# Two mixing slots handed to expert weights earlier, and an undivided gather, in a two-layer trunk kernel

## What is computed

```python
for l in range(DEPTH):                       # 2 layers; x is 256 x 1024, float32
    h = rms_norm(x, norm_mix_g[l])
    x = x + token_mixers(h, ...)             # h @ w_in, three branches, gates, w_proj_*, w_out
    h = rms_norm(x, norm_ffn_g[l])
    x = x + hier_moe(h, ...)                 # top-1 of 4 groups, top-2 of its 8 experts, 32 experts
return rms_norm(x, norm_final_g)

# in token_mixers, for branches i = a, b, c
merged = g[i = 0] * (ya @ w_proj_a) + g[1] * (yb @ w_proj_b) + g[2] * (yc @ w_proj_c)
return merged @ w_out
# in hier_moe, for each expert e, on its tokens
hid = silu(xb @ w_gate[e]) * (xb @ w_up[e]);  out += (hid @ w_down[e]) * weight
```

## Time and profile before

| what | value |
|---|---|
| median of 3 runs | 1387.93 us (1385.76 to 1388.62) |
| the profiled execution, its own time | 1388.38 us |
| its span, first to last instruction | 1385.9 us |
| mean granted TensorE clock | 0.996 of full |
| TensorE busy | 1367.3 us, 99% |
| VectorE, ScalarE busy | 584.4 us, 386.0 us |
| moved by DMA | 490.26 MB, 354 GB/s over the span |
| waits of TensorE for a DMA | 0.9 us in all, once |

### The profile page before, as it was taken

The page is one execution under the profiler, slowest core; times in us unless marked ns, Lnnn a source line. Parts: engine busy times, 40 slices in busy tenths (PEclk is TensorE's granted clock), DMA queues, the critical chain, the costliest instruction groups (busy, mean ns, idle before and its releaser), DMA issues. The chain is left out here.

```text
span 1385.9 us, 18830 instructions
## 1 busy us (share of the span) xinstructions
PE 1367.3 (99%) x7801; PEld 803.3 (58%) x7801; DVE 584.4 (42%) x945; ACT 386.0 (28%) x707; POOL 16.6 (1%) x44
## 2 busy tenths in 40 slices
PE   9999999999999999999999999999999999999997
PEld 8899888544444444444488988884444444444442
DVE  7796646632222222222278956466222222222223
ACT  6555443211111111111164553441111111111112
POOL 0000000100000000000000000010000000000000
PEclk9999999999999999999999999999999999999999
DMA  9645668999999999999975557599999999999996
GB/s 307 225 166 184 245 227 313 413 405 427 426 427 428 428 426 427 429 426 420 406 239 187 213 186 269 184 381 397 420 424 429 428 427 427 428 426 429 424 421 256
DMA packets 89676, 490.26 MB, mean 354 GB/s; under 512 B 10686, under 2 KB 13816, under 8 KB 58872
## 3 DMA queue, kind: packets, MB, share of 16 engines
q1 hardware_dynamic: 89488, 489.03, 87.9%
q10 hardware_dynamic: 104, 0.03, 0.0%
HBM read 487.99 MB, written 1.05 MB: 353 GB/s over the span
## 5 line engine op out<-in xcount | busy, mean ns | idle before, releaser
L2172 PE MATMUL psB<-slots,uT 128*64 128x512 f32 x2016 | 455.7, 595 | 0.3 <-DVE uT L1588 0.2
L2172 PEld LDWEIGHTS psB<-slots,uT 128*64 128x64 f32 x2016 | 140.3, 137 | 263.8 <-issue 259.9
L2182 PE MATMUL psC<-slots,ybT_plain 128*64 128x512 f32 x1024 | 233.0, 598 | 1.6 <-DMA slots<-in_expert_w_down_dram 0.9
L1249 DVE TENSOR_TENSOR parts<-slots,parts 128x2048 fp32r<-128x2048 f32 (+1 forms) x80 | 177.7, 2249 | 70.1 <-ACT parts L1006 69.2
L1006 ACT ACTIVATE parts<-slots 128x2048 fp32r<-128x2048 f32 (+1 forms) x80 | 148.3, 1888 | 98.0 <-PE psB L1817 52.5
L1645 DVE TENSOR_TENSOR x<-x,psA 128x1024 f32<-128x1024 f32 x60 | 73.3, 1222 | 211.9 <-PE psA L2222 211.9
L1113 ACT ACTIVATE rel_parts<-psC 128x512 fp32r<-128x512 f32 x62 | 37.1, 598 | 385.5 <-PE psC L2182 210.5
L1817 PE MATMUL psB<-parts,hT_parts 128*128 128x512 f32 x448 | 139.0, 391 | 0.9 <-DVE tmp L1526 0.5
L2182 PEld LDWEIGHTS psC<-slots,ybT_plain 128*64 128x64 f32 x1024 | 68.8, 136 | 117.5 <-issue 111.3
L1588 DVE TENSOR_TENSOR uT<-psA,g_ffn 128x512 f32<-128x512 f32 x64 | 44.3, 692 | 163.1 <-PE psA L2133 162.8
L1817 PE MATMUL psA<-parts,hT_parts 128*128 128x512 f32 x320 | 99.5, 392 | 0.0
(11 more groups left out here) (373 smaller groups left out, 1379.1 us busy)
## 6 DMA issues: line engine op xcount, KB each, us to landing
slots<-in_expert_w_down_dram SPq DMA_DIRECT2D x44, 2048.0 KB, 22.5
slots<-in_expert_w_gate_dram SPq DMA_DIRECT2D x40, 2048.0 KB, 22.9
slots<-in_expert_w_up_dram SPq DMA_DIRECT2D x40, 2048.0 KB, 21.7
slots<-in_w_in_dram SPq DMA_DIRECT2D x56, 1024.0 KB, 5.2
slots<-in_expert_w_gate_dram SPq DMA_DIRECT2D x44, 1024.0 KB, 10.5
slots<-in_expert_w_up_dram SPq DMA_DIRECT2D x42, 1024.0 KB, 10.5
slots<-in_expert_w_down_dram SPq DMA_DIRECT2D x28, 1024.0 KB, 10.7
slots<-in_expert_w_down_dram SPq DMA_DIRECT2D x24, 512.0 KB, 10.4
```

Source lines behind the costliest of these rows:

```text
L1249: v.tensor_tensor(low_part, mix_slot(i), high_part, ALU.subtract).then_inc(low_dve, 1)
L2172: ins = te.matmul(psB[j * BLK:(j + 1) * BLK, o, :], xT[:, 4 * half + c, j * BLK:(j + 1) * BLK], w, start=half == 0 and c == order[0], stop ...
L2182: ins = te.matmul(psC[j * BLK:(j + 1) * BLK, n, :], hidT[:, 2 * k + c, j * BLK:(j + 1) * BLK], w[:, c, n * 512:(n + 1) * 512], start=k == ...
```

## The change

Three things are edited. Raw slots: from use 32 on there are four instead of five; slot 17 is loaded with expert weights at the loop's step for use 32. High slots: from use 32 on there are three instead of four, so that `high` waits for use i - 3; slot 2 is loaded with expert weights at the step for use 33. The end of the loading program is adapted: `load_raw(35)` goes, and slots 12, 13, 15, 16 and 11, 9, 10 are loaded behind uses 36 to 39. Gather: all six terms of `gather(1)` stand ahead of the first down half.

```diff
-    FEWER_FROM = 30
+    FEWER_FROM, LEAST_FROM = 30, 32
     def raw_before(i):
-        return i - (RAWS if i < FEWER_FROM else RAWS - 1)
+        return i - (RAWS if i < FEWER_FROM else RAWS - 1 if i < LEAST_FROM else RAWS - 2)
+    HIGHS_FROM = 32
+    def high_before(i):
+        return i - (HIGHS if i < HIGHS_FROM else HIGHS - 1)
     def high_slot(i):
+        while i >= HIGHS_FROM:
+            i = high_before(i)
         return HIGH_AT[(i + HIGHS - MIX_SLOTS % HIGHS) % HIGHS]
@@ sync_program, loop over the uses
                     if i == FEWER_FROM:
                         load_raw(FEWER_FROM - RAWS)
+                    if i == LEAST_FROM:
+                        load_raw(LEAST_FROM - RAWS + 1)
+                    if i == HIGHS_FROM + 1:
+                        wait_used(sp, l, HIGHS_FROM - HIGHS)
+                        load_rest(2)
+                        load_early(2)
@@ sync_program, behind the loop
                 def load_high(i):
                     wait_used(sp, l, i)
-                    if high_slot(i) in FIRST:
-                        load_rest(high_slot(i))
-                        return
                     load_main(high_slot(i))
                 load_first(2)
-                load_raw(MIX_SLOTS - 5)
                 for i in range(MIX_SLOTS - 4, MIX_SLOTS):
                     if i == MIX_SLOTS - 1:
                         load_early(0)
-                        load_early(2)
-                    load_high(i)
+                    if i > MIX_SLOTS - HIGHS:
+                        load_high(i)
                     load_raw(i)
@@ scalar_program, high
                         if i >= HIGHS:
-                            wait_used(act, l, i - HIGHS)
+                            wait_used(act, l, high_before(i))
@@ tensor_program, pair
                     if gather_next:
-                        gather(1, terms=range(0, 2))
+                        gather(1)
                     pe.wait_ge(hidT_act, g * 2 + 1)
                     down(i, 0, tail)
-                    if gather_next:
-                        gather(1, terms=range(2, len(GATHER_TERMS)))
                     pe.wait_ge(hidT_act, g * 2 + 2)
                     down(i, 1, tail)
```

## The result

The changed kernel takes 1403.64 us (median of 4 runs, 1401.88 to 1404.77) against 1387.05 us before (4 runs): a ratio of 1.0113, 95% interval 1.0100 to 1.0126, so it is 15.7 us slower. Forecast were 1395.6 us in a range of 1388.5 to 1399.0, 7.7 us slower: the direction was right, the size half of what came, and the time lies outside the range. The profiled execution took 1401.88 us with a span (first to last instruction) of 1397.8 us, 11.9 more than before. The spans of the four runs are 1397.8, 1398.9, 1400.9 and 1401.7 us, by their median 14.0 us above the 1385.9 us of the profile of before; what is left of the 15.7 is time outside the span (3.1 to 4.1 us in these four runs, 2.5 in that profile) and scatter.

The account below looks back on a forecast made before the run. TensorE and the weight queue were taken to end both layers level, so the later decides: the queue's +2.7 and +1.2 a layer, +7.7 us together, takes the profiled 1388.4 to 1396.1, hence 1395.6 us for the runs; range 1388.5 to 1399.

Parts of the forecast that it names:

- What bounds the kernel: Expert stage: TensorE and the weight queue end both layers level within a microsecond; a gain on one alone is worth almost nothing.
- Part 1: Mixing stage: use 37's rounding waits for projection 34 and delays `merged_part(0)`, stalling TensorE before use 36 4.6 us a layer.
- The later waits: ScalarE's use 39 behind use 36 and `merged_part(1)` behind 39: no cost while 0.9 us of spare lasts.
- Part 2: TensorE behind the stall: its clock falls to half, costing 1.2 us a layer, bounds 0 and 2.4.
- Part 3: Raw slots and loads: the weight queue is late by 2.7 us a layer, 1.2 more if the clock falls.
- The walk up to slot 18: Queue followed at 2.5 us a slot from slots 6, 7 to 18: ends at about 951 instead of 948.3 us.
- Part 4: Expert pairs, undivided gather: TensorE gains 0.31 us a pair, 4.3 us a layer, 2.8 at the least.
- The sum: Per layer TensorE +1.5, queue +3.9; the later decides: +3.8 and +3.9, together +7.7 us.
- A: TensorE's clock stays up: the stall is there but nothing behind it runs at half rate; 1393.2 us, chance 0.25.
- B: Queue keeps the two early slots' 4.9 us in full, TensorE is the bound; 1387.9 to 1390.2 us, chance 0.12.
- C: ScalarE between 893.7 and 899.7: use 37's rounding doesn't hold up `merged_part(0)`, no stall; 1378.6 us, chance 0.08.
- D: Gather's order changes nothing on TensorE, which is then at +5.8 us a layer; 1398.8 us, chance 0.08.

Follow-up runs that it names:

- r_only: Kernel before with the four raw slots alone (slot 17 to expert weights at use 32), high slots and gather as they were: 1400.22 us, ratio 1.0078.
- s_only: Changed kernel with the gather divided again, so only the slots changed: 1403.22 us, ratio 1.0104 against the kernel before.
- a_spin20: Changed kernel with 20 small float32 matmuls into an unused tile in front of use 36: 1397.40 us, ratio 1.0065 against the kernel before.
- a_order: Changed kernel in which ScalarE rounds use 37 behind the merged sum's first half: 1390.16 us, ratio 1.0017 against the kernel before.
- h_only: Kernel before with the three high slots alone (slot 2 to expert weights at use 33), raw slots and gather unchanged: 1403.59 us, ratio 1.0101.
- a_spin: Changed kernel with 36 small float32 matmuls into an unused tile in front of use 36: 1405.47 us, ratio 1.0124 against the kernel before.
- l_before: Kernel before with the middle pairs' down-matrix loads bringing 3/4 of their bytes, gather divided: 1386.21 us, ratio 0.9979.

## Why the prediction was right in direction and wrong in size

- **What bounds the kernel** (queue and TensorE level at the end of both layers): right. The gather alone gave nothing, and 7.8 us with a lighter queue.
- **Part 1, the stall**: right in mechanism, place and nearly in size: 4.6 forecast, 4.8 and 5.1 measured, `merged_part(0)` 0.27 us later than forecast (906.56 against 901.55 + 4.74 = 906.29). The later waits cost nothing, as forecast. I called 4.6 the upper end; it wasn't. And I took the raw load's landing "ahead of the new 899.73" as no cost, where it is a second cause of nearly the same size, hidden behind the first, that `r_only` brought out.
- **Part 2, the clock**: right that it falls in both layers, the size was low. 1.2 us a layer forecast, 1.4 and 2.7 in the profiled execution, up to 3.0 in that of `s_only`; so the bound of 2.4 a layer was too small as well. `a_spin20` gives 4.4 us in all by the spans and 6.2 by the timed runs, instead of 2.4.
- **Part 3, the queue**: this is the step that failed. The walk up to slot 18 was right: 2.7 + 1.2 = 3.9 us late forecast, 5.5 measured in layer 1, and 1.5 of the 1.6 between them is the clock's 2.7 for my 1.2. Wrong was "From there to the end of the layer the queue is full, so this shift stays". The windows that it rests on are 907 to 931 and 1000 to 1290; the dip at 961.5 to 963 lay between them. The 1.9 us a layer by which I let the queue come back on TensorE (5.8 us less 3.9) was lost between slots 18 and 28, part of it already ahead of the dip. So the end moves by the whole lateness of the first pair: +6.5 and +7.2 us instead of +3.8 and +3.9.
- **Part 4, the gather**: 0.31 us a pair forecast, 0.30 measured, and worth nothing at the end, as the sum had it. That the 0.30 us are the two changes of type is my reading; no run parts them from the dividing of the down halves. The later release that I let vanish "into a queue that is full" fell on the one place where it wasn't.
- **The sum**: 6.5 + 7.2 = 13.7 us for the profiled execution, of which a luckier start took 1.8 (the clock fell near 9.9 us before and not after), 11.9 in the span. The 13.7 are 6.0 us above the forecast's 7.7: the queue's lost 1.9 us twice makes 3.8, the clock 1.7 (4.1 for 2.4), the stalls 0.7 (9.9 for 9.2), less small terms. The timed runs say 15.7. The profiled one has the shortest span of the four, the others have 1 to 4 us more; with their mean clocks at 0.992 to 0.993 against 0.994, and a span of 1401.7 us in the profile of `s_only`, which had half clock for 6.8 us in both layers, it is likely more of part 2. How often the clock stays down for 3.4 us and how often for 6.8 behind the same hole was not measured and stays open, and so does what is left of the 15.7 outside the spans.
- **The rivals**: A (clock up) gave 1393.2 and is nearly `a_spin20`'s case, 1397.4: the same error of the queue in it, +5.3 forecast and +9.1 measured. B and C fall with `a_order`; the stall was C's point of decision, and without it the kernel still wouldn't be faster. D, the gather without effect on TensorE, falls by the pairs of 27.09 us.

## What to carry to other kernels

- A buffer taken out of a rotation lengthens a wait, and the wait counts with everything behind it in its engine's program order. Follow that order first: here one rounding held back a merge that wasn't part of the change at all, and moving it behind the merge took away 13 of 15.7 us.
- A full prefetch ring can't be filled earlier. If the queue runs dry once after the early loads, look for that point over the whole stage window by window; here what was gained before it was lost there, and the lateness of the first consumer was paid in full.
- Where a stall of TensorE can't be avoided, try matmuls of just its length in it: 20 of them won 4 to 6 us here, 36 won nothing.

## What the hardware showed that I had not expected

- Behind a hole of 4.6 to 4.9 us TensorE's granted clock was 0.50 for 3.4 us in two cases (layer 0 of the changed kernel and of `h_only`) and for 6.8 us in four (`s_only` twice, layer 1 of the changed kernel and of `h_only`), with dense work behind the hole. Behind `r_only`'s holes of 3.3 and 4.1 us it was 3.4 and 6.8 us. 20 matmuls in the hole kept it at 1.00 behind it (4.4 us by the spans, 6.2 by the timed runs).
- The clock also fell where nothing of the change was near: in the kernel before at 934.92 us, ahead of layer 1's first pair (3.41 us at 0.50, TensorE busy all the time), and not at that place in `a_order`, `a_spin` and `l_before`.
- 16 bf16 matmuls between the float32 down halves cost 0.98 us of their own and 0.30 us more than the same matmuls in front of them, pair after pair (27.39 against 27.09 us).
